# A decoder layer on one core: the four norm weight columns placed ahead of both halves of the transposed activations in on-chip memory

## What is computed

```python
xn = rms_norm(h, attn_norm);  proj = xn @ w_in            # six groups of 512 columns
h = h + concat(moba_attention(...), stick_breaking_attention(...)) @ w_out
xf = rms_norm(h, ffn_norm)                                # PEER, 8 heads, 128 x 128 experts
s1, s2 = (xf @ w_query) halves @ sub_keys;  top 16 of each, top 16 of the pairs -> e_idx, gates
hid = gelu(xf . u_table[e_idx]);  h = h + sum(gates * hid * v_table[e_idx])
h = h + sigmoid(rms_norm(h, ple_norm) @ w_ple_gate) * (p @ w_ple)
```

## Time and profile before

| | |
|---|---|
| median of three runs | 962.65 us |
| the profiled execution, its own time | 962.73 us |
| its span in the profile | 961.0 us |
| TensorE busy | 949.7 us, 99% |
| VectorE, ScalarE, GpSimd busy | 72%, 64%, 35% |
| HBM traffic | 172.08 MB moved by the DMA queues, mean 179 GB/s |

### The profile page before, as it was taken

The page is one execution under the profiler, slowest core; times in us unless marked ns, Lnnn a source line. Parts: engine busy times, 40 slices in busy tenths (PEclk is TensorE's granted clock), DMA queues, the critical chain, the costliest instruction groups (busy, mean ns, idle before and its releaser), DMA issues.

```text
span 961.0 us, 19174 instructions
## 1 busy us (share of the span) xinstructions
PE 949.7 (99%) x6222; PEld 863.7 (90%) x6222; DVE 692.4 (72%) x1389; ACT 610.5 (64%) x1034; POOL 331.6 (35%) x148
## 2 busy tenths in 40 slices
PE   8999999999999999999999999999999999999998
PEld 5987889999999999999999998888888888888877
DVE  6747763999996888988888885555555555566763
ACT  7578664366676888888888885555445544556543
POOL 0002230178888777777777773000000000000000
PEclk9999999999999999999999999999999999999999
DMA  9770353045555544445454445555566666555521
GB/s 335 269 286 1 140 226 132 2 165 186 188 184 176 176 160 169 158 169 169 159 174 157 171 169 183 196 196 187 194 234 237 239 239 228 193 193 196 190 94 44
DMA packets 46459, 172.08 MB, mean 179 GB/s; under 512 B 5043, under 2 KB 8540, under 8 KB 44892
## 3 DMA queue, kind: packets, MB, share of 16 engines
q1 hardware_dynamic: 46284, 171.40, 52.0%
q10 hardware_dynamic: 144, 0.28, 0.1%
HBM read 169.55 MB, written 2.11 MB: 179 GB/s over the span
## 4 chain that ended last, share of the span: by engine, by line
PE 91%; DVE 4%; issue 2%; DMA 2%; ACT 1%; SPq 1%; POOL 1%; DVEq 0%; ACTq 0%; POOLq 0%
PE bank L1207 14%; PE bank L1206 14%; PE bank L1208 14%; PE pair L1520 12%; PE pair L1523 12%; PE pair L1522 12%; PE pair L1481 3%; PE pair L1236 1%; PE pair L1234 1%; PE pair L1235 1%; DMA w_raw<-w_in 1%; PE bank L1563 1%; PE bank L1236 1%; PE bank L1564 1%; PE bank L1565 1%
## 5 line engine op out<-in xcount | busy, mean ns | idle before, releaser
L583 ACT ACTIVATE t_hi<-t_raw 128x1024 fp32r<-128x1024 f32 x256 | 270.3, 1056 | 166.6 <-DMA t_raw<-v_chunks 162.6
L1178 POOL TENSOR_TENSOR t_lo<-t_raw,t_hi 128x1024 fp32r<-128x1024 f32 x130 | 311.5, 2409 | 144.0 <-ACT t_hi L583 143.9
L1207 PE MATMUL bank<-xt_lo,t_hi 128*128 128x256 f32 x1024 | 287.5, 281 | 0.0
L1206 PE MATMUL bank<-xt_hi,t_hi 128*128 128x256 f32 x1024 | 287.0, 280 | 0.2 <-POOL t_lo L1178 0.2
L1208 PE MATMUL bank<-xt_hi,t_lo 128*128 128x256 f32 x1024 | 286.5, 280 | 0.0
L910 DVE TENSOR_TENSOR t_lo<-t_raw,t_hi 128x1024 fp32r<-128x1024 f32 x126 | 154.4, 1225 | 136.7 <-ACT t_hi L583 136.5
L1520 PE MATMUL pair<-t_hi,g_hi 128*128 128x512 f32 x512 | 199.5, 390 | 0.1
L1522 PE MATMUL pair<-t_lo,g_hi 128*128 128x512 f32 x512 | 199.2, 389 | 0.0
L1523 PE MATMUL pair<-t_hi,g_lo 128*128 128x512 f32 x512 | 199.2, 389 | 0.0
L1208 PEld LDWEIGHTS bank<-xt_hi,t_lo 128*128 128x128 f32 x1024 | 193.1, 189 | 0.0
L1206 PEld LDWEIGHTS bank<-xt_hi,t_hi 128*128 128x128 f32 x1024 | 192.8, 188 | 0.4 <-POOL t_lo L1178 0.4
(11 more groups left out here) (270 smaller groups left out, 1293.8 us busy)
## 6 DMA issues: line engine op xcount, KB each, us to landing
t_raw<-u_chunks SPq DMA_DIRECT2D x128, 512.0 KB, 3.2
t_raw<-v_chunks SPq DMA_DIRECT2D x128, 512.0 KB, 3.3
w_raw<-w_query SPq DMA_DIRECT2D x4, 2048.0 KB, 7.6
w_raw<-w_in SPq DMA_DIRECT2D x3, 2048.0 KB, 10.9
w_raw<-w_out SPq DMA_DIRECT2D x2, 2048.0 KB, 8.3
wg_raw<-w_gate SPq DMA_DIRECT2D x8, 512.0 KB, 4.8
w_raw<-w_in SPq DMA_DIRECT2D x7, 512.0 KB, 8.4
w_raw<-w_in SPq DMA_DIRECT2D x2, 1024.0 KB, 10.3
```

The costliest lines, as they stand in the source:

```text
L583: nc.scalar.activation(t_hi[:, q % RING, :], t_raw[:, q % RING, :], ACT.Copy).then_inc(t_hi_ready, 1)
L1178: nc.gpsimd.tensor_tensor(t_lo[:, q, :], t_raw[:, q, :], t_hi[:, q, :].bitcast(f32), ALU.subtract).then_inc(t_lo_pool, 1)
L1206: mm(dst, ah, bh, start=(c == 0), stop=False)
L1207: mm(dst, ah, bl, start=False, stop=False)
```

## The change

The table of sizes, from which the places follow, is written in another order. h is first in both; gains and xt_lo stay neighbours.

```diff
-        sizes = dict(h=2 * D, xt_hi=DC * SEQ, gains=4 * DC, xt_lo=DC * SEQ, cst=4 * P, qkg=32, stats=192)
+        sizes = dict(h=2 * D, gains=4 * DC, xt_lo=DC * SEQ, xt_hi=DC * SEQ, cst=4 * P, qkg=32, stats=192)
```

## The result

The changed kernel takes 968.16 us (median of 20 runs, 967.59 to 975.33) against 962.98 us of 20 runs of the kernel before: ratio 1.0053, 95% interval 1.0042 to 1.0064. It is slower, where 950.5 us was forecast. The profiled execution took 968.73 us. A few executions of these kernels had a lower granted clock (0.949 to 0.993, most others 0.999 or 1.0) and took some 5 to 10 us longer, which moves a median little, and three of 1580, 1951 and 3358 us are left out of the ratios.

What follows compares the result with a forecast made beforehand. TensorE's own working rate was taken to bound the kernel. Gains of 10.4 + 2.2 + 1.3 us less 1.7 us of waiting gave 12.2 us, hence 950.5 us; its own range was 946 to 956 us, 8-in-10 range 946 to 970.

Steps and rivals of the forecast that it cites:

- What bounds the kernel: Whole kernel: TensorE's own working rate is the limit, busy 949.7 of 961.0 us at full clock.
- The pause of 16 columns: Matmul streams: time above the column count comes in units of 16 columns, 6.67 ns at 2.4 GHz.
- Equal distances even out the three lines: Three matmuls of a product: recorded alike, some 276 ns in the u stage, 389 ns in the output projection.
- the settled spacing: u stage, 256 moving columns at steady distance 128: one 6.67 ns pause per matmul, 113.3 ns instead of 117.5.
- a jump costs a pause: Matmul streams: each change of distance between successive matmuls costs about one 6.67 ns pause.
- the 10.4 us gained in the u stage: u stage: 2486 settled matmuls each save 4.2 ns, 10.4 us together.
- the 3.1 us of the groups ahead of it: Ahead of the u stage: column groups save 2.2 us, 512-column groups through the output projection 0.9 us.
- the 512-column groups: K_M to output projection: 204 settled matmuls go from 230.9 to 226.7 ns, saving 0.9 us; final gate 0.4 us.
- Rival 3: u stage, column and 512-column groups: distance 128 is bad, u matmuls take 120.0 ns, total 972.4 us; chance 0.26.
- Settling within nine matmuls: Read at v-stage entry: a steady distance finds the cheap rhythm after about nine matmuls, 231 ns becoming 227 ns.
- The 1.7 us at step 36: u stage: TensorE gains 4.3 us against 2.6 us of slack, so waits 1.7 us for VectorE's choice.
- The rule that the prediction set against itself: Trainium skill: PE never waits and weight loads take no matmul read bandwidth; then the sum is 0, time 962.7 us.

## Why the prediction was wrong, point by point

- **What bounds the kernel: right.** TensorE's own rate moved, in 5.2 of the 6.0 us of span; 0.7 us more lie idle in the v stage.
- **The pause of 16 columns: right.** 120.0 ns in the run with both halves at 0, 113.3 ns at 192 and 233 ns in the v stage with shifted weights are 2, 1 and 3 pauses on 106.7, 106.7 and 213.3 ns. The settled number need not be whole, though: 118.8 ns at 128 is 1.8 pauses.
- **Equal distances even out the three lines: right** in the changed kernel (394 to 395; 281, 281, 281).
- **The step that failed: the settled spacing.** "I take one pause ... because rows 3 to 5 are the nearest" carried three assumptions. One was that a jump costs a pause with 256 columns as it seemed to with 512; the run with both at 0 has no jump in the u stage and costs 2.5 ns a matmul more than the jumping one. The second was that a settled relation is the cheap one at every distance; the third, "a whole number a matmul is one", fell with the 1.8 pauses at 128. Measured in its place: 118.8 ns at 128 where 113.3 was put, so the 10.4 us gained in the u stage were 3.8 us lost, the 3.1 us of the groups ahead of it 1.4 us lost, and the 512-column groups went to 394 to 395 ns, not 389. The rows quoted had settled relations at distance 0 alone. The earlier trace rows were also misread: the weights are at 0, 0, 128, so each of the three matmuls has a change of distance before or behind it, not two of them; the two longer ones are those with a change behind them.
- **Rival 3 had the direction right, and the mechanism in part.** It held 128 itself to be the bad distance and priced two pauses each, 120.0 ns and 972.4 us; it was 118.8 ns and 968.2 us. In the u stage 128 is not the bad one: both halves at 0 cost 120.0 ns, more than both at 128. What the change gave up there is the jumping 0, 128, 0 at 117.5 ns, for a settled relation that costs more, as those at 0, 96 and 256 do too. Its argument for, the 282 ns of xt_lo in the earlier trace rows, was thin; the other, that the change leads away from the only settled distance seen, was the sound one, and held for the 512-column groups (395 for 389 ns with the v weights at 128).
- **Settling within nine matmuls: half right.** It was read from one entry. Distances 64 and 192 have two rhythms, and the stream stays in the one it has, for 26 steps on end at 192 before step 36, until other matmuls come between.
- **The 1.7 us at step 36: wrong too, as the run at 192 shows.** The changed kernel cannot test it, since TensorE comes there later than before. In the run at 192 TensorE comes to its transposes 4.9 us earlier (288.15 against 293.04 us) and does not stand idle. VectorE's last step starts 3.6 us earlier than in the earlier trace rows; it takes 1.87 us in place of 0.42 and ends 2.2 us earlier, at 288.20 us:

```profile
166.09 4.43 DVE L724 TENSOR_TENSOR w_lo<-w_raw,w_hi 128x4096 fp32r<-128x4096 f32 x1 [7.74 <-ACT w_hi L401]
...
286.33 1.87 DVE L1003 TENSOR_TENSOR gate<-gate,stats 128x256 f32<-128x256 f32 x1
```

  The chain began 1.2 us earlier and reached its last step 2.4 us quicker, of which the longer last step took 1.45 us back. That VectorE "is full from there on the earlier trace rows, so it does not come earlier" took its start and the length of its instructions as fixed. What made them shorter or longer was not tested.
- **The rule that the prediction set against itself.** The Trainium skill, SBUF — State Buffer, Who interferes with whom, says that PE never waits on anyone; the Trainium skill, TensorE: Matmul & The Clock Gate, in its step on LDWEIGHTS, says that the weight load takes no read bandwidth from the running matmul. The kernel with shifted v weights has the same instructions and waits, only the address of two weight buffers differs, and the v stage goes from 226.0 to 232.6 ns a matmul. By the rule that address should cost nothing, so in this form (fp32r, 128 weight columns under 256 or 512 moving, granted clock 1.0) the trace disagrees with it, and the measurement decides. Whether it is the weight load that holds the moving columns up is not shown.

What stays open: why the number of pauses goes with the distance as it does (120.0 ns at 0, 118.8 at 128, 0 and 96 alike), what picks the rhythm of the first 40 steps at 64 and 192, why gates at another distance turn it over, and whether distances finer than 32 bytes do better. That the pauses are meetings of the two readers in one part of the memory is my reading; the runs show only that they depend on the distance between the two operands modulo 256 bytes.

## What to carry to other kernels

When TensorE is full and its matmuls are spaced 6 to 10% over their column count, try the distance between moving operand and weights, modulo 256 bytes, as a tuning knob, and measure it: 0 was best with 512 moving columns and among the worst with 256, where 192 was best. Do not carry the good distance from one shape to another, and look at the spacing of single steps as well as at the mean, since one relation can have two rhythms. Then look at what runs between the steps: a few matmuls at another distance can turn the rhythm over. Here both halves at 192 gives 953.25 us, 1% under the kernel before and 1.5% under the changed one, for 512 bytes of padding in each partition; part of that rests on the first 40 steps having caught the good rhythm.

## What the runs showed of the hardware that I had not expected

The address of an operand changes the rate of a matmul stream by up to 6% (113.3 to 120.0 ns with 256 moving columns) while the other engines have the same instructions. Only the relative place counts, as far as tried: a shift of all buffers by 128 bytes left 2215 matmuls in a stretch that had 2214. And the stream has a memory: the same instructions at the same addresses run steadily at 113.3 or at 117.8 ns, and each of 64 groups of four matmuls at another distance switched from one to the other.
